# Three matmuls of 256 columns into one bank in place of 512 + 256 into two: the projections of a two-block transformer kernel

## The chip, the cores and the metric

One core of one Trainium2 chip runs the whole kernel. The metric is device time in microseconds. Before the change it is 3007.14 us, the median of three runs from 3000.47 to 3011.03. The engines are named as in the profile: PE is TensorE's matmul side, PEld its weight loads, DVE is VectorE, ACT is ScalarE, POOL is GpSimd, SP the engine that issues most DMAs.

## The reference, cut to what matters

The input is one sequence of 256 tokens with 2048 features, in fp32. The first block has a recurrent branch (width 2816), 16 heads of stick-breaking attention, a gated mixture, a feed-forward part of width 5632 and a gated extra input; then come two hybrid layers with differential attention, dilated attention and a convolution branch. Nearly all arithmetic is products of the 256 tokens with large weight matrices:

```
proj = h @ w_in[i]                                   # 2048 x 15872
y_r = ... @ w_rnn_out[i];  y_a = ... @ w_attn_out[i];  x = x + mix @ w_o[i]
gu = h @ w_ffn_gu[i];  x = x + (silu(g) * u) @ w_ffn_down[i]
ple_gate = sigmoid(rmsnorm(x, g_ple[i]) @ w_ple_gate[i])
proj = x @ w_in                                      # in each of the two hybrid layers
y = concatenate([ya, yb, yc], -1) @ w_out
```

All of them are to be right to more than one matmul in the fast fp32 format gives, so weights and activations are split.

## The kernel before

Activations lie with features on the 128 partitions and the 256 tokens (T) along the free side. The weight stream is cut in units: four k-tiles of 128 rows by 256 output columns (COLS), 512 KB, which SP loads into one of four slots of RAW. ACT makes the high part, WH, by a copy in the format fp32r (L594), DVE the low part, WL = RAW - WH (L1065), or POOL in a few units (L508). The activations in XH and YH are kept as two halves of 512 columns: columns 0 to 255 the high part, 256 to 511 the low part (L1090).

A group is 256 output columns over all k. For each k-tile and each half j of 128 output columns, PE does two matmuls with 128x128 stationary weights: WH against all 512 columns of x (L1755), and WL against the 256 high columns (L1757). The second adds into the upper half of the same bank, so a bank ends with WH*x_high in its lower 256 columns and WH*x_low + WL*x_high in its upper 256. The half j has a bank of its own; with two groups in turns (par) all four banks of the tile PG are used. When a group is complete, DVE evacuates it (L1078): a sum over the two halves of both banks, 1024 values per partition in, 512 out. PE waits, before it opens a group, for the evacuation of the group two before it (s_evac), and before each unit for WL (s_lo); where the activations of a phase are fresh, for them too (s_op).

The phases follow one another in the order of the program: attn (4 turns of 6 groups), gate_a, attn_out, x_r, gate_r, g_r, rnn_out, w_o, three pairs gu and down, ple, and for each of the two layers conf, dil, diffa, diffb, outa, outb and ln. Turn 0 of a phase is written out, the others run in a loop of the engine. Between groups a hook issues the small matmuls of attention, norms and the block-diagonal gates (L1851) into another tile, PX; transposes are L1779 and L1910. Nothing reorders instructions; each engine runs its own list, and semaphores tie them.

The stored program of PE has 10,459 matmuls before and 15,435 after; the hardware trace lists each with its weight load, and loops repeat them.

Of the kernel before, what the change touches and what calls it, by code (L numbers as in the profile page):

```python
# [23 lines left out]
T = 256  # L24
# [160 lines left out]
def program(nc, A, turns, real):  # L185
# [4 lines left out]
    AX = mybir.AxisListType.X  # L190
    ctx = ExitStack()
    with ctx:
        def sb(name, shape, dt=fp):
            return ctx.enter_context(nc.sbuf_tensor(name, shape, dt))
# [3 lines left out]
        WH = sb("WH", [P, SLOTS, UK, COLS], fr)  # L198
        WL = sb("WL", [P, SLOTS, UK, COLS], fr)
# [13 lines left out]
        PG = ctx.enter_context(nc.psum_tensor("PG", [P, 4, 512], fp))  # L213
# [120 lines left out]
        for l in range(2):  # L334
# [13 lines left out]
            out = [Group(wo, DC, 0, 0, YH, part=slice(1, U), closes=False),  # L348
                   Group(wo, DC, COLS, 0, YH, part=slice(1, U), closes=False, ahead=1),
                   Group(wo, DC, 0, 0, YH, part=slice(0, 1), opens=False, seen=2 * U - 1),  # L350
                   Group(wo, DC, COLS, 0, YH, part=slice(0, 1), opens=False)]
# [73 lines left out]
        s = Semaphores(*(ctx.enter_context(nc.semaphore("s_" + name)) for name in NAMES))  # L425
# [616 lines left out]
        def _(dve):  # L1042
            c = Counts(dve, "dve", turns, real)
            V_ = nc.vector
# [27 lines left out]
            def evacuate(grp, dst=None):  # L1072

                par = c.n.get("group", 0) % 2

                dve.wait_ge(s.unit, c.next("seen", grp.seen))
                out = G[:, par, :, :] if dst is None else dst
                V_.reduce_sum(out, PG[:, 2 * par:2 * par + 2, :].rearrange("p b (h t) -> p b t h", h=2), AX)\  # L1078
                    .then_inc(s.evac, 1)
                c.add("group")  # L1080
                dve.wait_ge(s.evac, c.value("group"))
                return Gf[:, par, :]
# [20 lines left out]
            def a_q(grp, i):  # L1103
                evacuate(grp, two(QR[:, 0, :]))

            def a_k(grp, i):
                evacuate(grp, two(QR[:, 1, :]))
                from_act()
                done(V_.scalar_tensor_tensor(QR[:, 0, :], QR[:, 0, :], der(D_QG), SQ2[:, 0, :], ALU.mult, ALU.mult))

            def a_v(grp, i):
                evacuate(grp)
                from_act()
                V_.scalar_tensor_tensor(QR[:, 1, :], QR[:, 1, :], vec("k_gain"), SQ2[:, 1, :], ALU.mult, ALU.mult)\
                    .then_inc(s.ready, 1)
                dve.wait_ge(s.ready, c.next("ready"))
# [614 lines left out]
        def _(pe):  # L1731
            c = Counts(pe, "pe", turns, real)
            mm = nc.tensor.matmul

            def group(grp, fresh=(), mid=None):


                par = (c.n.get("group", 0) + grp.ahead) % 2
                if grp.opens and c.n.get("group", 0) >= 2:

                    pe.wait_ge(s.evac, c.value("group", grp.ahead - 1))
                units = grp.units()
                for n, (k0, nk) in enumerate(units):
                    slot = c.n.get("unit", 0) % SLOTS

                    pe.wait_ge(s.lo, c.value("unit", 1))
                    if n < len(fresh) and fresh[n]:

                        pe.wait_ge(s.op, c.next("op", fresh[n]))
                    for kk in range(nk):  # L1750
                        x = grp.X[:, grp.base + k0 + kk, :]
                        for j in range(2):
                            b = 2 * par + j
                            cs = slice(P * j, P * j + P)
                            mm(PG[:, b, :], WH[:, slot, kk, cs], x, start=grp.opens and n == 0 and kk == 0,  # L1755
                               stop=False)
                            last = mm(PG[:, b, T:2 * T], WL[:, slot, kk, cs], x[:, 0:T], start=False,  # L1757
                                      stop=grp.closes and n == len(units) - 1 and kk == nk - 1)
                    last.then_inc(s.unit, 1)
                    c.add("unit")  # L1760
                    if mid and n in mid:
                        mid[n]()
                if grp.closes:
                    c.add("group")
# [230 lines left out]
            for q in range(DC // 2):  # L1995
# [7 lines left out]
                for e in range(2):  # L2003
                    for b in range(NB):
                        at = T * e + P * b
                        src = D * b + P * (2 * q + e)
                        last = nc.tensor.transpose(PG[:, q % 4, at:at + P], Fv[:, src:src + P], IDENT)
                last.then_inc(s.tp, 1)
                if q == 7:
                    ready()  # L2010
                    for b in range(NB):
                        last = mm(PX[:, 0, P * b:P * b + P], ONES, Gf[:, 1, P * b:P * b + P], start=True, stop=True)
                    last.then_inc(s.ss, 1)
            for ph in phases:
                if ph.name in between:
                    between[ph.name]()
                    continue
                hook = after.get(ph.name)

                def turn(i):  # L2020
                    for j, grp in enumerate(ph.body):
                        first = isinstance(i, int) and i == 0
                        group(grp, ph.fresh.get(j, ()) if first else (),
                              {0: diff_sum} if j == 1 and ph.name[:4] == "outa" else None)
                        if hook:
                            hook(i, j)
                turn(0)
                c.loop(1, ph.n, turn)

            for q in range(DC // 2):  # L2030
# [5 lines left out]
                for e in range(2):  # L2036
                    for b in range(NB):
                        at = T * b + P * e
                        last = nc.tensor.transpose(PG[:, q % 4, at:at + P], XRES[:, 2 * q + e, P * b:P * b + P],
                                                   IDENT)  # L2040
# [27 lines left out]
```

## Time and profile before

| | |
|---|---|
| median of the runs | 3007.14 us |
| span of the profiled execution | 3001.7 us |
| PE busy | 2922.9 us, 97% |
| PE's weight loads busy | 2534.9 us, 84% |
| DVE busy | 2130.3 us, 71% |
| ACT busy | 1411.3 us, 47% |
| POOL busy | 421.6 us, 14% |
| mean granted clock of PE | 0.989 of full speed |

The profiled execution's own time, what lies around its span included, is not listed apart; the three runs lie 1.2 us below to 9.3 us above its span. A busy PE is not a PE at its peak: durations of matmuls overlap, because the next starts while the pipeline of the last one drains. What a matmul costs is read from one start to the next.

### The profile page before, as it was taken

How to read it: one execution, taken by the hardware profiler on the slowest of the kernel's cores; microseconds unless marked ns; L12 is line 12 of the kernel's file. 1: busy time of each engine (PE TensorE's matmuls, PEld its weight loads, DVE VectorE, ACT ScalarE, POOL GpSimd, SP SyncE). 2: the span in 40 equal slices, each digit the busy share in tenths (PEclk: the TensorE clock that was granted, in tenths of full speed). 3: DMA queues.
4: the chain of work that ended last, by engine and by line, in shares of the span. 5: the costliest groups of instructions: out<-in, count | busy, mean ns of one | idle time of the engine just before them, and what ended most of it. 6: DMA issues, size and time to landing. Idle time of an engine off the chain costs nothing.

```text
span 3001.7 us, 45154 instructions
## 1 busy us (share of the span) xinstructions
PE 2922.9 (97%) x16516; PEld 2534.9 (84%) x16516; DVE 2130.3 (71%) x2372; ACT 1411.3 (47%) x1671; POOL 421.6 (14%) x382
## 2 busy tenths in 40 slices
PE   7999999999999999999999999999999997999997
PEld 6888888888888888888888888888888886888786
DVE  6666656776677677766666667776887786797777
ACT  5666643346654444443443344544444545434453
POOL 1000000203010000000000000116921100980110
PEclk9999999999999999999999999999999998999998
DMA  5545556653456556666565565565554554555453
GB/s 182 165 147 165 161 179 193 203 186 115 126 182 190 184 191 201 189 195 192 170 196 179 187 192 180 181 193 179 168 178 147 166 182 127 172 176 177 134 168 112
DMA packets 516869, 518.39 MB, mean 173 GB/s; under 512 B 17425, under 2 KB 514685, under 8 KB 516733
## 3 DMA queue, kind: packets, MB, share of 16 engines
q1 hardware_dynamic: 512357, 508.32, 54.1%
q0 software_dynamic: 3296, 5.56, 0.7%
q10 hardware_dynamic: 1080, 2.69, 0.3%
q8 instruction: 86, 1.41, 0.2%
q14 instruction: 50, 0.41, 0.0%
HBM read 514.39 MB, written 2.12 MB: 172 GB/s over the span
## 4 chain that ended last, share of the span: by engine, by line
PE 59%; DVE 9%; ACT 3%; issue 2%; DVEq 0%; POOL 0%; ACTq 0%; POOLq 0%
PE PG L1755 38%; PE PG L1757 19%; DVE WL L1065 3%; ACT WH L594 1%; DVE G L1078 1%; DVE MIX L1507 1%; DVE MIX L1394 0%; DVE F L1078 0%; DVE XRES L1606 0%; DVE TT L1618 0%; DVE TT L1235 0%; PE PX L1803 0%; ACT YH L685 0%; ACT L746 0%; DVE MIX L1725 0%
## 5 line engine op out<-in xcount | busy, mean ns | idle before, releaser
L1755 PE MATMUL PG<-XH,WH 128*128 128x512 f32 x4864 | 1733.8, 401 | 32.7 <-DVE XH L1090 23.2
L1065 DVE TENSOR_TENSOR WL<-RAW,WH 128x1024 fp32r<-128x1024 f32 (+1 forms) x944 | 1131.7, 1232 | 451.6 <-ACT WH L594 441.7
L1757 PE MATMUL PG<-XH,WL 128*128 128x256 f32 x4864 | 1364.6, 281 | 0.0
L594 ACT ACTIVATE WH<-RAW 128x1024 fp32r<-128x1024 f32 (+1 forms) x972 | 992.3, 1049 | 781.8 <-PE PG L1757 549.7
L1755 PEld LDWEIGHTS PG<-XH,WH 128*128 128x128 f32 x4864 | 917.5, 189 | 263.2 <-issue 35.0
L1755 PE MATMUL PG<-YH,WH 128*128 128x512 f32 x2848 | 1000.9, 396 | 7.2 <-DVE YH L1090 3.7
L1757 PEld LDWEIGHTS PG<-XH,WL 128*128 128x128 f32 x4864 | 922.1, 190 | 4.6 <-issue 4.1
L1757 PE MATMUL PG<-YH,WL 128*128 128x256 f32 x2848 | 796.4, 280 | 0.0
L1755 PEld LDWEIGHTS PG<-YH,WH 128*128 128x128 f32 x2848 | 534.1, 188 | 135.7 <-issue 9.5
L1757 PEld LDWEIGHTS PG<-YH,WL 128*128 128x128 f32 x2848 | 537.3, 189 | 1.3 <-issue 1.2
L1078 DVE TENSOR_REDUCE G<-PG 128x512 f32<-128x1024 f32 x198 | 241.2, 1218 | 36.7 <-PE PG L1757 36.6
L508 POOL TENSOR_TENSOR WL<-RAW,WH 128x1024 fp32r<-128x1024 f32 x28 | 67.4, 2407 | 1122.0 <-ACT WH L594 1063.6
L523 POOL MEMSET AL<- 128x1024 f32 x22 | 21.2, 965 | 674.3 <-DVE G L1078 507.9
L557 POOL TENSOR_SCALAR F<-MIX,VEC 128x256 f32<-128x256 f32 x56 | 78.8, 1407 | 0.0
L557 POOL TENSOR_SCALAR MIX<-MIX,VEC 128x256 f32<-128x256 f32 x56 | 73.5, 1312 | 5.5
L1394 DVE SCALAR_TENSOR_TENSOR MIX<-MIX,VEC 128x256 f32<-128x256 f32 x120 | 63.0, 584 | 6.4 <-DVE F L1420 1.9
L565 POOL TENSOR_TENSOR RT<-RT,F 128x256 f32<-128x256 f32 x56 | 62.8, 1122 | 0.0
L1851 PE MATMUL PX<-F,AL 128*128 128x256 f32 x280 | 61.7, 379 | 0.0
L1851 PEld LDWEIGHTS PX<-F,AL 128*128 128x128 f32 x280 | 52.6, 190 | 7.2
L821 ACT ACTIVATE F<-F,DER 128x128 f32<-128x128 f32 x64 | 29.2, 457 | 58.7 <-DVE DER L1409 57.6
L685 ACT ACTIVATE XH<-TT 128x512 f32 (+1 forms) x22 | 13.9, 632 | 89.4 <-DVE TT L1293 89.4
L565 POOL TENSOR_TENSOR RT<-RT,MIX 128x256 f32<-128x256 f32 x56 | 50.1, 895 | 4.7
(261 smaller groups left out, 1499.0 us busy)
## 6 DMA issues: line engine op xcount, KB each, us to landing
RAW<-in_w_in_dram SPq DMA_DIRECT2D x488, 512.0 KB, 4.7
RAW<-in_w_ffn_gu_dram SPq DMA_DIRECT2D x176, 512.0 KB, 4.6
RAW<-in_w_ffn_down_dram SPq DMA_DIRECT2D x88, 512.0 KB, 4.6
RAW<-in_w_out_dram SPq DMA_DIRECT2D x64, 512.0 KB, 4.6
RAW<-in_w_rnn_out_dram SPq DMA_DIRECT2D x40, 512.0 KB, 4.5
RAW<-in_w_attn_out_dram SPq DMA_DIRECT2D x32, 512.0 KB, 4.5
RAW<-in_w_o_dram SPq DMA_DIRECT2D x32, 512.0 KB, 4.7
RAW<-in_w_ple_gate_dram SPq DMA_DIRECT2D x32, 512.0 KB, 4.8
```

The costliest lines, as they stand in the source:

```text
L508: nc.gpsimd.tensor_tensor(WL[:, slot, :, :], RAW[:, slot, :, :], WH[:, slot, :, :].bitcast(fp), ALU.subtract).then_inc(s.lo, 1)
L557: ins = nc.gpsimd.tensor_scalar(to, HC[:, ch, tap + 2:tap + 2 + T], vec("conv_dw_2", (l * TAPS2 + tap) * CONVC + ch), None, ALU.mult)
L565: ins = nc.gpsimd.tensor_tensor(CB[:, ch, :], CB[:, ch, :], PT[ch % 2], ALU.add)
L594: nc.scalar.activation(WH[:, u % SLOTS, 0:nk, :], RAW[:, u % SLOTS, 0:nk, :], ACT.Copy)\
L821: last = nc.scalar.activation(S4[:, x, lo:up], S4[:, x, lo:up], ACT.Exp, bias=der(D_RED + 2 * x + b), accum_out=der(D_RED + 8 + 2 * x + b))
L1065: V_.tensor_tensor(WL[:, u % SLOTS, 0:nk, :], RAW[:, u % SLOTS, 0:nk, :], WH[:, u % SLOTS, 0:nk, :].bitcast(fp), ALU.subtract).then_inc(s. ...
L1078: V_.reduce_sum(out, PG[:, 2 * par:2 * par + 2, :].rearrange("p b (h t) -> p b t h", h=2), AX)\
L1394: ins = V_.scalar_tensor_tensor(CA[:, ch, :], src, vec("conv_dw_2", at), CA[:, ch, :], ALU.mult, ALU.add)
L1507: ins = V_.scalar_tensor_tensor(CA[:, ch, :], CA[:, ch, :], vec("conv_ln_g_2", CONVC * l + ch), PN[:, T:2 * T], ALU.mult, ALU.mult)
L1755: mm(PG[:, b, :], WH[:, slot, kk, cs], x, start=grp.opens and n == 0 and kk == 0, stop=False)
L1757: last = mm(PG[:, b, T:2 * T], WL[:, slot, kk, cs], x[:, 0:T], start=False, stop=grp.closes and n == len(units) - 1 and kk == nk - 1)
L1851: last = mm(PX[:, j % 4, T * m:T * m + T], BDS[:, i % 8, m, at:at + P], XC[:, i, :], start=i == users[j][0], stop=i == users[j][-1])
```

## The change

PG's one bank per group takes both halves: half j has columns 256 j to 256 j + 255. The matmul of WH against 512 columns is written as two of 256 columns, high part and low part of x, both into the same 256 columns of the bank, and WL against the high part adds there too. Only the very first matmul of a group opens the bank. The evacuation is a copy of 512 values instead of a sum over 1024. Banks 2 and 3 are no longer used by the groups.

```
-                V_.reduce_sum(out, PG[:, 2 * par:2 * par + 2, :].rearrange("p b (h t) -> p b t h", h=2), AX)\
-                    .then_inc(s.evac, 1)
+                V_.tensor_copy(out, two(PG[:, par, :])).then_inc(s.evac, 1)
...
+                        end = grp.closes and n == len(units) - 1 and kk == nk - 1
                         for j in range(2):
-                            b = 2 * par + j
+                            to = PG[:, par, T * j:T * j + T]
                             cs = slice(P * j, P * j + P)
-                            mm(PG[:, b, :], WH[:, slot, kk, cs], x, start=grp.opens and n == 0 and kk == 0,
-                               stop=False)
-                            last = mm(PG[:, b, T:2 * T], WL[:, slot, kk, cs], x[:, 0:T], start=False,
-                                      stop=grp.closes and n == len(units) - 1 and kk == nk - 1)
+                            mm(to, WH[:, slot, kk, cs], x[:, 0:T],
+                               start=grp.opens and n == 0 and kk == 0 and j == 0, stop=False)
+                            mm(to, WH[:, slot, kk, cs], x[:, T:2 * T], start=False, stop=False)
+                            last = mm(to, WL[:, slot, kk, cs], x[:, 0:T], start=False, stop=end and j == 1)
```

On PE, at the head of the loop of the attention phase (PG is the accumulator, XH the activations, WH and WL the high and low weights; the first row is the loop's wait for the evacuation), there stands before:

```order
L1746 ISA [waits s_evac]
L1755 MATMUL PG<-XH,WH 128x512 [waits s_lo]
L1757 MATMUL PG<-XH,WL 128x256
L1755 MATMUL PG<-XH,WH 128x512
L1757 MATMUL PG<-XH,WL 128x256
```

and now:

```order
L1745 ISA [waits s_evac]
L1755 MATMUL PG<-XH,WH 128x256 [waits s_lo]
L1757 MATMUL PG<-XH,WH 128x256
L1758 MATMUL PG<-XH,WL 128x256
L1755 MATMUL PG<-XH,WH 128x256
L1757 MATMUL PG<-XH,WH 128x256
L1758 MATMUL PG<-XH,WL 128x256
```

Three matmuls stand where two stood, each with a weight load of its own; the waits are the same. The body of this loop has 450 rows before and 643 after, and is the longest of all loops.

On DVE, in the same loop, around the evacuation of a group (F is its target), before:

```order
L1065 TENSOR_TENSOR WL<-RAW,WH 128x1024 [waits s_hi]
L1078 TENSOR_REDUCE F<-PG 128x512 [waits s_unit]
L1081 REGISTER_ALU
L1070 REGISTER_ALU [waits s_evac]
L1109 SCALAR_TENSOR_TENSOR F<-F,DER 128x512 [waits s_act]
```

and now:

```order
L1065 TENSOR_TENSOR WL<-RAW,WH 128x1024 [waits s_hi]
L1078 COPY F<-PG 128x512 [waits s_unit]
L1080 REGISTER_ALU
L1070 REGISTER_ALU [waits s_evac]
L1108 SCALAR_TENSOR_TENSOR F<-F,DER 128x512 [waits s_act]
```

Only the kind of the instruction changes there; nothing is moved on DVE, and ACT, POOL and SP have the same lists as before.

## Rows read from the trace of the kernel before

**Rows 1.** The page: span and busy time of each engine.
```profile
span 3001.7 us, 45154 instructions
PE 2922.9 (97%) x16516; PEld 2534.9 (84%) x16516; DVE 2130.3 (71%) x2372; ACT 1411.3 (47%) x1671; POOL 421.6 (14%) x382
```

**Rows 2.** Costliest groups: shapes, count | busy us, mean ns | idle before.
```profile
L1755 PE MATMUL PG<-XH,WH 128*128 128x512 f32 x4864 | 1733.8, 401 | 32.7 <-DVE XH L1090 23.2
...
L1757 PE MATMUL PG<-YH,WL 128*128 128x256 f32 x2848 | 796.4, 280 | 0.0
```

**Rows 3.** The chain that ended last, by engine and by line.
```profile
PE 59%; DVE 9%; ACT 3%; issue 2%; DVEq 0%; POOL 0%; ACTq 0%; POOLq 0%
PE PG L1755 38%; PE PG L1757 19%; DVE WL L1065 3%; ACT WH L594 1%; DVE G L1078 1%; DVE MIX L1507 1%; DVE MIX L1394 0%; DVE F L1078 0%; DVE XRES L1606 0%; DVE TT L1618 0%; DVE TT L1235 0%; PE PX L1803 0%; ACT YH L685 0%; ACT L746 0%; DVE MIX L1725 0%
```

**Rows 4.** PE's timeline near 1000 us: start us, duration us.
```profile
1000.04 0.40 PE L1755 MATMUL PG<-YH,WH 128*128 128x512 f32 x1
1000.29 0.28 PE L1757 MATMUL PG<-YH,WL 128*128 128x256 f32 x1
1000.41 0.40 PE L1755 MATMUL PG<-YH,WH 128*128 128x512 f32 x1
...
1005.71 0.40 PE L1755 MATMUL PG<-YH,WH 128*128 128x512 f32 x1
```

**Rows 5.** PE's timeline near 450 us.
```profile
450.07 0.28 PE L1757 MATMUL PG<-YH,WL 128*128 128x256 f32 x1
450.19 0.39 PE L1755 MATMUL PG<-YH,WH 128*128 128x512 f32 x1
450.42 0.27 PE L1757 MATMUL PG<-YH,WL 128*128 128x256 f32 x1
450.53 0.40 PE L1755 MATMUL PG<-YH,WH 128*128 128x512 f32 x1
...
455.74 0.39 PE L1755 MATMUL PG<-YH,WH 128*128 128x512 f32 x1
```

**Rows 6.** PE's waits: waited for: us in total, times, longest us.
```profile
PE PG L1755 <- DVE XH L1090: 23.2, 3, 11.2
PE PG L1755 <- DVE WL L1065: 12.1, 7, 5.0
PE PX L1910 <- DVE F L1459: 9.2, 2, 4.6
...
PE PG L1755 <- DVE YH L1090: 3.7, 2, 1.9
```

**Rows 7.** PE's timeline before a stall at 2314 us.
```profile
2314.56 0.28 PE L1757 MATMUL PG<-XH,WL 128*128 128x256 f32 x1
2319.46 0.90 PE L1910 MATMUL PX<-MATS,F 128*128 128x128 f32 x3 [4.62 <-DVE F L1459]
```

**Rows 8.** Durations of the two lines, ns: min/median/max, first and last start.
```profile
L1755 PE MATMUL PG<-YH,WH x2848: 391/395/799, 441.2 to 2971.1; 128*128 128x512 f32 x190
...
L1757 PE MATMUL PG<-YH,WL x2848: 274/280/284, 441.4 to 2971.3; 128*128 128x256 f32 x190
```

**Rows 9.** PE's timeline in the stretch at half clock, 28 us.
```profile
28.53 0.63 PE L1755 MATMUL PG<-XH,WH 128*128 128x512 f32 x1
28.96 0.41 PE L1757 MATMUL PG<-XH,WL 128*128 128x256 f32 x1
29.17 0.63 PE L1755 MATMUL PG<-XH,WH 128*128 128x512 f32 x1
```

**Rows 10.** A line of matmuls in true fp32.
```profile
L1851 PE MATMUL PX<-F,AL 128*128 128x256 f32 x280 | 61.7, 379 | 0.0
```

**Rows 11.** PE's weight loads near 2115 us: ten loads for ten transposes.
```profile
2115.43 0.69 PEld L1910 LDWEIGHTS PX<-MATS,F 128*128 128x128 f32 x6
2116.09 0.47 PEld L1779 LDWEIGHTS PX<-MATS,G 128*128 128x128 f32 x4
2116.53 0.19 PEld L1755 LDWEIGHTS PG<-XH,WH 128*128 128x128 f32 x1
```

**Rows 12.** DVE's evacuations and two kinds of copies from PSUM.
```profile
L1078 DVE TENSOR_REDUCE G<-PG 128x512 f32<-128x1024 f32 x198 | 241.2, 1218 | 36.7 <-PE PG L1757 36.6
...
L1078 DVE TENSOR_REDUCE F<-PG 128x512 f32<-128x1024 f32 x40 | 48.6, 1215 | 0.0
L1078 DVE TENSOR_REDUCE MIX<-PG 128x512 f32<-128x1024 f32 x12 | 14.6, 1219 | 0.1
...
L1637 DVE COPY XRES<-PG 128x512 f32<-128x512 f32 x8 | 5.5, 692 | 9.7 <-PE PG L2007 9.7
L1119 DVE COPY F<-PX 128x512 f32<-128x512 f32 x8 | 5.5, 692 | 0.3
```

**Rows 13.** PE in the phase g_r: stretch, busy (matmuls), clock, DMA, GB/s.
```profile
835.00:905.00 70.00, 69.59 (x388) 1.00 0.57 182
```

**Rows 14.** DMA queue of instruction fetches: packets, MB, share.
```profile
q8 instruction: 86, 1.41, 0.2%
```

**Rows 15.** DMA issues of the first weights: count, size, us to landing.
```profile
RAW<-in_w_in_dram SPq DMA_DIRECT2D x488, 512.0 KB, 4.7
```

## The prediction

> **What bounds the kernel now.** I read the page from the top. PE is busy 97% of a 3001.7 us span, DVE 71%, ACT 47% [rows 1]. The table of costly groups shows that nearly all of PE's time is two lines, L1755 (512 moving columns against WH) and L1757 (256 against WL), 4864 + 2848 = 7712 of each [rows 2]. The chain of waits gives PE 59%, those two lines 57%, with the split L1065 at 3% and the evacuation L1078 at 1% behind them [rows 3]. So I need what one pair of matmuls costs from start to start, not the printed durations, which overlap. The timeline gives it: 16 pairs from 1000.04 to 1005.71 us, 354 ns each [rows 4], and 16 pairs from 450.19 to 455.74, 347 ns each [rows 5]. The kernel alternates between these two rhythms, whatever DVE and ACT do; I take 350. 7712 x 0.350 = 2699 us, 90% of the span. Stalls are few: the list of who waited for whom has 23.2 us in 3 waits for XH, 12.1 in 7 for WL, 9.2 in 2 for F, 3.7 in 2 for YH [rows 6]; one row of the timeline is such a wait, 4.62 us [rows 7].
>
> **The change, PE's part.** Per k and half: before one WH load, 512 columns, one WL load, 256 columns. After: WH load, 256, the same WH load again, 256, WL load, 256. Moving columns stay 768; loads and matmuls go from two each to three each, so 7712 of both are added. The sum is therefore 7712 x (three 256-column steps - 350 ns).
>
> What is a 256-column step worth? Start to start it is 0.11 or 0.12 us, and a 512-column one 0.23 to 0.25 [rows 4, 5]. Finer: the durations have medians 395 and 280 ns [rows 8]; if both contain the same pipeline tail c, then 395 + 280 - 2c = 350, c = 162.5, and the steps are 232 and 117 ns. Minimum and maximum of L1757, 274 and 284, give 111 and 121. So three steps are 351 ns, bounds 333 and 364; against 350 that is +1 ns, +8 us, with ends -130 and +110 us. I take +8 since the median is where the rows lie, and the two ends are single steps of a rhythm that never stay (111 follows 118 or so).
>
> Is the step of 117 a real price of 256 columns when three come in a row? Three things in the rows speak for it. It already contains a load of WH behind it, and the load starts as the matmul starts. It does not shrink or grow when nothing follows: the last L1757 before a stall of almost 5 us lasts the same 0.28 [rows 7]. And it is in proportion: 256 columns more cost 232 - 117 = 115 ns, as much as the first 256, so next to nothing is left as a fixed price per matmul. At half clock (1.2 GHz, at 28 to 29 us) the steps are 0.43 and 0.21, which is one column per cycle with no extra [rows 9]; at 2.4 GHz 768 columns would be 320 ns, so the 30 ns above that are a limit that shows only at the full clock. If it is by column the change is free; if it is by matmul, it is a rival (below). True-fp32 matmuls of 256 columns, two passes each, last 379 ns, so 216 with the tail off, against 213 of pure columns [rows 10]: a matmul with its load need not cost more than 3 ns extra.
> The Trainium skill says, under TensorE: Matmul & The Clock Gate, Part 1, that a warm matmul carries about 2.5 ns on top of its columns. By that rule the added matmul alone costs 7712 x 2.5 ns, an estimate of +19 us, where the steps of the rows give +8; the true-fp32 rows agree with the size.
>
> Accumulation: WL's 256 columns already follow at once on WH's last 256 into the same place of the bank, so three in a row on one place add no nearer pair of writes. The banks: group and next group still use different ones, and what PE waits for before it opens a group (two groups back) is the same.
>
> Loads: three in 350 ns. Ten transposes in a row, each with its load of 128 columns, start 0.11 us apart [rows 11], so a load fits in 109 to 110 ns and hides in 117. If that cover were gone, each load would show whatever it exceeds 117 by; nothing here shows such an excess.
>
> **DVE's part.** The evacuation becomes a copy of 512 from one bank in place of a sum of 1024 over two. There are 250 (198 + 40 + 12) at 1.218 us; copies of 128x512 from PG and PX take 0.692 [rows 12]. That takes 0.526 us from each, 131 us of DVE work. Almost all of it lies beside PE's matmuls and is worth nothing. It is worth something in two places. First, in the stalls at phase ends, where the last evacuation stands ahead of what PE waits for: of the 14 waits just named, the two for F and the one of 11.2 us at the start have none in front [rows 6], which leaves 11, 11 x 0.5 = 5 us. Second, where the chain runs from evacuation to activation to the next split and PE is just short of work: from 835 to 905 us PE ran 388 matmuls in 70 us, 361 ns a pair [rows 13], so 11 ns above the rhythm; over the eleven groups of g_r, 352 pairs, that is 4 us, and 0.526 per group (5.8 us in all) covers it. Late next there is PE's own rhythm. Sum -9 us, bounds 0 (all hidden behind the next wait) and -20 (the stalls of 48 us in rows 6 lose one evacuation each, and some splits come earlier too).
>
> **Instruction fetch.** The program's matmuls go from 10,459 to 15,435. The fetch queue moved 86 blocks, 1.41 MB, in the whole run [rows 14]. That is 67 bytes for each of the stored 2 x 10,459 loads and matmuls but 43 for each of the 2 x 16,516 executed; I read it as the program fetched once, with loops running from what is held. All loops but one stay, after the change, below the 450-row body of the attention loop of before; that one grows to 643 rows. If it no longer fitted, its three turns would each fetch anew: at about 5 us from issue to landing, as the weights need [rows 15], no more than 15 us. The cost I take is 0.
> The Trainium skill (Runtime: NRT & Kernel Launch, Instruction fetch mechanics) gives PE room for 2048 instructions, in blocks of 256; 86 blocks hold 22,016, which agrees with the program once. By it 643 rows with their loads, near 1290, still fit. No run here shows the limit.
>
> **The sum.** +8 - 9 + 0 = -1 us against 3001.7 of span; the median of the runs is 3007.1, 5.4 above that span, and runs spread over 10 us, so I forecast 3005.
>
> **Rivals.**
> 1. A fixed price per matmul or weight swap. If the 30 ns above 320 are 15 per matmul, and the recorded starts hide it, a triple is 320 + 45 = 365: +15 x 7712 = +116 us, 3120. For it: the extra exists only at the full clock, where a load and the columns compete for less time. Against it: 232 against 117 is in proportion, and true-fp32 matmuls carry 3 ns. It ends slower; it decides from a fixed part of about 2 ns on (2 x 7712 = 15 us). Chance 0.17.
> 2. PE's sequencer. Six instructions per 350 ns are 58 each, before four, 88 each. Twenty (ten loads, ten transposes) took 1.10 us, 55 each [rows 11], limited perhaps by the array, so the sequencer can do 58 but the margin is unknown for longer runs. At 62 ns each the triple is 372, +22 x 7712 = +170 us, 3175. Chance 0.06. The Trainium skill (TensorE: Matmul & The Clock Gate, Part 1) has about 62 ns per MATMUL when the sequencer decodes in software; if this held for loads also, it is this case, and the 55 in the trace speaks against it.
> 3. The steps settle lower. There is a rhythm of 347 now in half the places; equal steps could lock there or at 3 x 115 = 345 throughout: -5 x 7712 = -39 us, and -9 of DVE, 2957. For it: the rhythm is regular to the nanosecond and depends on order. Against it: nothing says that the equal steps take the better one. Chance 0.15.
> 4. The relief of DVE is worth nothing, since each stall ends with ACT's or a weight's part; then +8 stands alone, 3013. This is within my own case.
>
> **Chances.** My case (steps of 115.5 to 118, so PE between -27 and +31 us, DVE -9) has 0.62; it is 2975 to 3035 by itself, likeliest 3005. A difference under 0.3% (9 us) cannot be told from none. Within my case faster, same and slower are 0.21, 0.25 and 0.16. With rival 3 faster is 0.36; with 1 and 2 slower is 0.39; same 0.25. The range holds my case, rival 3 and most of rival 1: 2955 to 3120.
>
> **What would show it.** Right: starts of L1755, L1757 and L1758 0.11 to 0.12 apart, three of them 0.345 to 0.355; durations near 280 on all three lines; L1078 at 0.69 us; DVE near 66% busy; the fetch queue near 126 blocks. In g_r the pair at 350. Rival 1 or 2: steps of 0.12 to 0.124, durations of 285 or more, and for rival 2 loads that start well after the matmul before them. Refetching: far more than 126 blocks. Wrong altogether: PE's clock leaving 2.4 GHz more often than the few short stretches of now, or new stalls for WL.

## The result and the profile after

The changed kernel takes 3059.53 us (median of four runs, 3057.14 to 3061.33) against 3006.83 us before (four runs of it by now): a ratio of 1.0184, 95% interval 1.0165 to 1.0204, so about 55 us slower. The forecast was 3005 us, which is no change, with a range of 2955 to 3120. The time lies in the range, and the slowdown was missed, though of the three chances the one for slower, 0.39, was the largest.

Three words recur below. A step is the time from one matmul's start to the next one's; a pair is the two matmuls of the kernel before, a triple the three of the changed one, each for one k-tile and one half of the output columns.

The page after: span and busy times (they answer to [rows 1]), the fetch queue ([rows 14]), the chain ([rows 3]), one of the groups of matmuls ([rows 2]) and DVE's evacuation ([rows 12]).

```profile
span 3059.5 us, 60578 instructions
...
PE 2993.1 (98%) x24228; PEld 2958.3 (97%) x24228; DVE 2006.9 (66%) x2372; ACT 1419.4 (46%) x1671; POOL 426.2 (14%) x382
...
q8 instruction: 125, 2.05, 0.3%
...
PE 68%; DVE 4%; ACT 1%; issue 1%; ACTq 0%; DVEq 0%
PE PG L1755 22%; PE PG L1758 22%; PE PG L1757 22%; DVE MIX L1506 1%; DVE XRES L1605 0%; DVE TT L1617 0%; PE PX L1803 0%; PE PX L1910 0%; PE PX L1901 0%; PE PX L1773 0%; DVE WL L1065 0%; PE PX L1779 0%; ACT WH L594 0%; PE PX L1804 0%; PE PX L1887 0%
...
L1757 PE MATMUL PG<-YH,WH 128*128 128x256 f32 x2848 | 805.9, 283 | 0.0
...
L1078 DVE COPY G<-PG 128x512 f32<-128x512 f32 x198 | 135.6, 685 | 45.8 <-PE PG L1758 45.8
```

DVE has lost 123 us of work, near the 131 expected, and the chain now runs through PE for 68% where it was 59%, and through DVE for 4% where it was 9%: the relief is there. A 256-column matmul lasts 283 ns in the mean, 3 ns more than the 280 of [rows 2]. The timeline of the changed kernel's PE (start us, duration us) gives the step from start to start:

```profile
471.04 0.28 PE L1755 MATMUL PG<-YH,WH 128*128 128x256 f32 x1
471.16 0.28 PE L1757 MATMUL PG<-YH,WH 128*128 128x256 f32 x1
471.28 0.28 PE L1758 MATMUL PG<-YH,WL 128*128 128x256 f32 x1
471.40 0.28 PE L1755 MATMUL PG<-YH,WH 128*128 128x256 f32 x1
...
472.84 0.28 PE L1755 MATMUL PG<-YH,WH 128*128 128x256 f32 x1
```

Fifteen steps in 1.80 us are 120.0 ns each, 360.0 a triple, and so it is in every undisturbed stretch of the program. The pair of before lasts 350.2 on average over the undisturbed stretches of its trace. So the 3 ns of each step over the 117 that I had read make the loss: 7712 x (360.0 - 350.2) = +76 us, less what the lighter evacuation gives back. The same stretch, 470 to 640 us, where both kernels run projections without a gap, shows it by counting; before, it is one of those with the faster rhythm, 347, so the difference is 13 ns there and not 10 (columns: stretch, busy us and number of matmuls, clock, DMA share, GB/s). Before:

```profile
470.00:640.00 170.00, 170.00 (x982) 1.00 0.63 194
```

and after:

```profile
470.00:640.00 170.00, 170.00 (x1420) 1.00 0.63 189
```

491 pairs before, 346 ns each, and 473 triples after, 359 (each count holds a few matmuls that hang over an edge). The clock is full in both; the loss is not a slower clock.

At half clock the changed kernel pays nothing extra, as before ([rows 9]): steps of 0.21 and 0.22 us, one column per cycle.

```profile
28.96 0.41 PE L1758 MATMUL PG<-XH,WL 128*128 128x256 f32 x1
29.17 0.41 PE L1755 MATMUL PG<-XH,WH 128*128 128x256 f32 x1
29.38 0.41 PE L1757 MATMUL PG<-XH,WH 128*128 128x256 f32 x1
29.60 0.41 PE L1758 MATMUL PG<-XH,WL 128*128 128x256 f32 x1
```

### The profile page after: what moved, and what is told of

It reads as the page before. It is cut to its first block, busy times and chain, and to the rows that moved or that the text cites. A ratio compares the mean times of both kernels' runs of the same rounds, so it can differ in the third digit from the quotient of the medians.

```text
span 3059.5 us, 60578 instructions
## 1 busy us (share of the span) xinstructions
PE 2993.1 (98%) x24228; PEld 2958.3 (97%) x24228; DVE 2006.9 (66%) x2372; ACT 1419.4 (46%) x1671; POOL 426.2 (14%) x382
## 4 chain that ended last, share of the span: by engine, by line
PE 68%; DVE 4%; ACT 1%; issue 1%; ACTq 0%; DVEq 0%
PE PG L1755 22%; PE PG L1758 22%; PE PG L1757 22%; DVE MIX L1506 1%; DVE XRES L1605 0%; DVE TT L1617 0%; PE PX L1803 0%; PE PX L1910 0%; PE PX L1901 0%; PE PX L1773 0%; DVE WL L1065 0%; PE PX L1779 0%; ACT WH L594 0%; PE PX L1804 0%; PE PX L1887 0%
## 5 line engine op out<-in xcount | busy, mean ns | idle before, releaser
L1755 PE MATMUL PG<-XH,WH 128*128 128x256 f32 x4864 | 1395.1, 287 | 27.8 <-DVE XH L1089 23.0
L1757 PE MATMUL PG<-XH,WH 128*128 128x256 f32 x4864 | 1380.8, 284 | 0.0
L1758 PE MATMUL PG<-XH,WL 128*128 128x256 f32 x4864 | 1380.7, 284 | 0.0
L1755 PEld LDWEIGHTS PG<-XH,WH 128*128 128x128 f32 x4864 | 938.5, 193 | 35.3 <-issue 32.0
L1757 PEld LDWEIGHTS PG<-XH,WH 128*128 128x128 f32 x4864 | 938.4, 193 | 4.8 <-issue 4.3
L1758 PEld LDWEIGHTS PG<-XH,WL 128*128 128x128 f32 x4864 | 938.0, 193 | 0.0
L1755 PE MATMUL PG<-YH,WH 128*128 128x256 f32 x2848 | 809.4, 284 | 3.8 <-DVE YH L1089 3.4
L1758 PE MATMUL PG<-YH,WL 128*128 128x256 f32 x2848 | 806.0, 283 | 0.0
L1757 PE MATMUL PG<-YH,WH 128*128 128x256 f32 x2848 | 805.9, 283 | 0.0
L1755 PEld LDWEIGHTS PG<-YH,WH 128*128 128x128 f32 x2848 | 546.7, 192 | 6.3 <-issue 5.5
L1757 PEld LDWEIGHTS PG<-YH,WH 128*128 128x128 f32 x2848 | 546.7, 192 | 1.3 <-issue 1.2
L1758 PEld LDWEIGHTS PG<-YH,WL 128*128 128x128 f32 x2848 | 546.7, 192 | 0.0
L1078 DVE COPY G<-PG 128x512 f32<-128x512 f32 x198 | 135.6, 685 | 45.8 <-PE PG L1758 45.8
```

The costliest lines, as they stand in the source:

```text
L1078: V_.tensor_copy(out, two(PG[:, par, :])).then_inc(s.evac, 1)
L1755: mm(to, WH[:, slot, kk, cs], x[:, 0:T], start=grp.opens and n == 0 and kk == 0 and j == 0, stop=False)
L1757: mm(to, WH[:, slot, kk, cs], x[:, T:2 * T], start=False, stop=False)
L1758: last = mm(to, WL[:, slot, kk, cs], x[:, 0:T], start=False, stop=end and j == 1)
```

## The experiments

**Which part of the change it is.** Two runs take the change apart. The first keeps the two banks and the sum, and only splits the matmul:

```
-mm(PG[:, b, :],        WH[..., cs], x,          start=..., stop=False)
+mm(PG[:, b, 0:T],      WH[..., cs], x[:, 0:T],  start=..., stop=False)
+mm(PG[:, b, T:2 * T],  WH[..., cs], x[:, T:2 * T], start=False, stop=False)
 last = mm(PG[:, b, T:2 * T], WL[..., cs], x[:, 0:T], ...)
```

> The matmul split alone: three matmuls of 256 columns, but into the two banks per group of the kernel before, and with its evacuation (a sum over 1024). In the changed kernel every step from one matmul's start to the next is 120 ns, 360 for a triple, where the pair took 350. If the price lies in the split (theories: a fixed part per matmul, a limit per weight load, a limit per instruction), the triple is 360 here too: 7625 to 7712 times 10 ns is +76 us, and since nothing is relieved on DVE the time is 3070 to 3085, slower than the changed kernel by what the lighter evacuation is worth (5 to 20 us). If the price lies in the accumulator (three matmuls in a row onto the same 256 columns of one bank), the triple falls back to 350 here and the time to 3000 to 3012.

Measured: 3069.47 us against 3003.51 before, ratio 1.0224 (1.0206 to 1.0242), and the steps are 120 ns here too, 1419 matmuls where the changed kernel has 1420:

```profile
470.00:640.00 170.00, 170.00 (x1419) 1.00 0.62 188
```

So the accumulator has no part in it; the split does it. The second run keeps the pair and only makes the evacuation light:

```
-V_.reduce_sum(out, PG[:, 2 * par:2 * par + 2, :].rearrange("p b (h t) -> p b t h", h=2), AX)
+V_.tensor_copy(out, two(PG[:, 2 * par, :]))
```

> The evacuation alone: the pair of matmuls of the kernel before, with a copy of 512 values from one bank in place of the sum over two (what the second half holds is left out). It shows what the relief of DVE is worth where PE has its old rhythm. By the prediction -9 us, so 2998; if all of it hides behind other waits 0; the rhythm of PE stays 347 or 353 ns a pair. If it moves more than 20 us, the relief also changes PE's rhythm.

Measured: 2989.87 us against 3003.51, ratio 0.9955 (0.9937 to 0.9974), 13.5 us faster (8 to 19). PE's waits in it, which answer to [rows 6]:

```profile
PE PG L1754 <- DVE XH L1089: 22.6, 3, 11.2
...
PE PG L1754 <- DVE WL L1065: 7.7, 4, 4.0
...
PE PX L1909 <- DVE F L1458: 7.3, 2, 3.6
...
PE PG L1754 <- DVE YH L1089: 3.7, 2, 1.9
```

48.2 us of such waits have become 41.3. And in g_r, where [rows 13] has 388 matmuls in 70 us, there are now 396, 354 ns a pair and not 361, which over 352 pairs is 2.6 us:

```profile
835.00:905.00 70.00, 69.94 (x396) 1.00 0.57 182
```

This run also shows that the rhythm of the pair is not a property of the place. From 470 to 640 us it has 965 matmuls, 352 ns a pair, where the run of before has 982, and from 1720 to 1800 it has 463 where the run of before has 455:

```profile
470.00:640.00 170.00, 170.00 (x965) 1.00 0.64 194
...
1720.00:1800.00 80.00, 80.00 (x463) 1.00 0.62 189
```

**What a step is made of.** A fixed price per matmul, a floor per weight load (a step can't be shorter than its load), or a floor per instruction: all three give 120. The next runs change one size at a time. First, the second matmul of each triple with half the moving columns:

```
-mm(to, WH[..., cs], x[:, T:2 * T], start=False, stop=False)
+mm(PG[:, par, T * j:T * j + 128], WH[..., cs], x[:, T:T + 128], start=False, stop=False)
```

> The changed kernel, with the second matmul of each triple (WH against the low part of x) cut to 128 moving columns; the other half of the tokens misses that product. Fixed part per matmul (columns at 2.4 GHz plus 13.3 ns, which gives 120 for 256 and 226.7 for 512): its step falls to 53.3 + 13.3 = 67 ns, the triple to 307, the time by 411 us to about 2650, as far as other engines let it. Limit per weight load (a step with a load of 128 columns can't be under 120) or per instruction (60 ns each): steps stay at 120, triple 360, time 3059.

Measured: 2994.29 us, a triple of 349 to 353 ns, by the stretch:

```profile
470.00:640.00 170.00, 170.00 (x1464) 1.00 0.63 194
...
900.00:1100.00 200.00, 200.00 (x1700) 1.00 0.61 191
```

Neither theory's number: 128 columns less save 7 to 11 ns, not 53 and not 0. The timeline shows why the three steps must be taken together:

```profile
449.90 0.28 PE L1755 MATMUL PG<-YH,WH 128*128 128x256 f32 x1
450.02 0.22 PE L1757 MATMUL PG<-YH,WH 128*128 128x128 f32 x1
450.08 0.34 PE L1758 MATMUL PG<-YH,WL 128*128 128x256 f32 x1
450.26 0.28 PE L1755 MATMUL PG<-YH,WH 128*128 128x256 f32 x1
```

L1758 is printed as starting 0.06 us after L1757, and then "lasts" 0.34 where it lasts 0.28 elsewhere. So its start was recorded early. That it then stood waiting for its load is likely, since e5 below has 112 ns from load to load, but it is not shown. In a stream of unequal matmuls the printed starts and durations move time from one to the other; only the sum is right.

Next, the same second matmul with 64 columns of weights in place of 128:

```
+mm(PG[0:64, par, T * j:T * j + T], WH[:, slot, kk, P * j:P * j + 64], x[:, T:2 * T], start=False, stop=False)
```

> The changed kernel, with the second matmul of each triple loading only 64 columns of WH as weights (64 of 128 output features get the product with the low part of x), still 256 moving columns. Fixed part per matmul: all steps stay 120. Limit per instruction: all stay 120. Limit per weight load: the step that hides this half load is no longer held by it and falls towards the 107 to 109 ns that 256 columns take, so the triple to about 347 and the time by 95 us to about 2965.

Measured: 2993.41 us, triple 350.0.

```profile
470.00:640.00 170.00, 170.00 (x1459) 1.00 0.63 195
```

The width of the load matters with moving columns and instructions unchanged, but this is a mixed stream again. So the following runs make all three matmuls alike (the first and last k-tile of a group keep their shapes):

```
+w_, m_ = (P, T) if first or last k-tile else (128, 128)     # then (64, 256), (64, 128), (32, 256)
+to = PG[0:w_, par, T * j:T * j + m_];  cs = slice(P * j, P * j + w_)
 mm(to, WH[..., cs], x[:, 0:m_]);  mm(to, WH[..., cs], x[:, T:T + m_]);  mm(to, WL[..., cs], x[:, 0:m_])
```

> The changed kernel with all three matmuls of a triple cut to 128 moving columns (the first and last k-tile of a group keep their shapes; the other half of the tokens misses the products), weights still 128 columns. The two runs before it left two theories: a floor per weight load, about 116 ns for 128 columns (W), and a floor per instruction, about 58 ns, two per step (I). Both expect steps of about 116, a triple near 349, though the columns alone would take 53 ns. If instead the steps fall to 70 or less, the price goes with the moving columns.

Measured: 3017.3 us; steps 111.7 ns (335.0 a triple), not the 116 of either theory.

```profile
449.94 0.27 PE L1761 MATMUL PG<-YH,WL 128*128 128x128 f32 x1
450.05 0.27 PE L1758 MATMUL PG<-YH,WH 128*128 128x128 f32 x1
450.16 0.27 PE L1760 MATMUL PG<-YH,WH 128*128 128x128 f32 x1
450.27 0.28 PE L1761 MATMUL PG<-YH,WL 128*128 128x128 f32 x1
```

With 128 weight columns a step doesn't fall below 112 ns, though its moving columns would take 53. That lies under 120: loads could keep up with the changed kernel. It also accounts for e3, whose triple would be 120.0 + 111.7 + 120.0 = 351.7, between the 349 and 353 measured. The mean clock of this run was 0.948 and not 0.989, which costs it time outside these steps, so its total says nothing on them.

> The changed kernel with all three matmuls loading 64 columns of weights, 256 moving columns each (half of the output features are not computed). W: loads take 60 ns or so and the moving columns decide: 107 to 109 ns a step, a triple of 320 to 327. I: still 116 a step, 349. If both the load and the columns get in each other's way, something between.

Measured: 2940.77 us; the durations of one line (ns, min/median/max):

```profile
L1760 PE MATMUL PG<-YH,WH x2848: 276/276/283, 434.1 to 2909.0; 128*64 128x256 f32 x163, 128*128 128x256 f32 x27
```

Uniform streams settle the tail of a duration too: 283 for a step of 120.0, so 163, and this median is a step of 113.3, 340.0 a triple. It is not 107 to 109, as theory W (a floor per load) had it, and not 116, as theory I (a floor per instruction) had it. 6.7 ns over the columns are left of 13.3. In e4 one such step beside two full ones should give 353.3; it had 350.0, and why is open. Half the weight columns also means results for half the partitions; no run separates the two.

> The changed kernel with 64 columns of weights and 128 moving columns in all three matmuls (three quarters of the products are left out). W: steps of 58 to 65 ns, since a half load takes about half. I: still 116, since there are two instructions in each step whatever their size. The time of the kernel will be set by DVE and ACT then, so the steps within a unit are what is read.

Measured: 2569.59 us; steps of 60 ns where PE doesn't wait. The total can't be compared, since PE now often waits for other engines and its mean clock is 0.903.

```profile
1251.73 0.22 PE L1760 MATMUL PG<-YH,WH 128*64 128x128 f32 x1
1251.79 0.22 PE L1761 MATMUL PG<-YH,WL 128*64 128x128 f32 x1
1251.85 0.22 PE L1758 MATMUL PG<-YH,WH 128*64 128x128 f32 x1
1251.91 0.22 PE L1760 MATMUL PG<-YH,WH 128*64 128x128 f32 x1
```

Two instructions, a load and a matmul, in 60 ns: a floor of 58 ns per instruction is out. And 60 is again the columns at 2.4 GHz, 53.3, and 6.7.

The next run goes the other way, from the kernel before: WL's matmul gets all 512 columns of x, so that every step moves 512.

```
-last = mm(PG[:, b, T:2 * T], WL[..., cs], x[:, 0:T], ...)
+last = mm(PG[:, b, :],       WL[..., cs], x,         ...)
```

> The kernel before with the WL matmul over all 512 columns of x (one product more than the result needs), so that PE runs 512 and 512, with a load of 128 columns under each. No load can be late there. If a 512-column step is its columns and a small fixed part, it is 213 + 3 = 216, the pair 432; if the step of 230 to 235 seen in the kernel before is the column rate of this format, the pair is 460 to 470; if what is added to the columns is paid per load (13 to 17 ns each), 453 to 460. Against 350 the first adds 630 us to the time, the second 850 to 925.

Measured: 3763.01 us; pairs of 453.3 in every undisturbed stretch, 226.7 a step. The durations and the count:

```profile
L1757 PE MATMUL PG<-YH,WL x2848: 387/389/402, 548.5 to 3730.7; 128*128 128x512 f32 x190
...
470.00:640.00 170.00, 170.00 (x753) 1.00 0.46 144
```

This is the run that decides. 512 columns are 213.3 ns at 2.4 GHz and cost 226.7; 256 are 106.7 and cost 120.0. The extra is 13.3 ns in both. It is paid per matmul with its load of 128 weight columns, whether 256 or 512 columns move. Every matmul here has a load of its own, so what a matmul without one would pay isn't shown. The pair of before should then cost 226.7 + 120.0 = 346.7, which is the faster of its two rhythms (347 in [rows 5]).

The last of the uniform streams loads 32 weight columns per matmul.

> The changed kernel with all three matmuls of a triple loading 32 columns of weights, 256 moving columns each (three quarters of the output features are not computed, but for the first and last k-tile of a group). Steps so far at 256 moving columns: 120.0 ns with 128 weight columns, 113.3 with 64; the columns alone are 106.7. If the extra goes with the width of the load, a quarter load adds 3.3 ns, a step of 110.0, a triple of 330. If it is a fixed part of 6.7 per matmul plus something that only a full load adds, the step stays 113.3, a triple of 340.

Measured: 2979.66 us. In some stretches steps of 113.3, as with 64 columns, in others up to about 117.8, never 110:

```profile
L1760 PE MATMUL PG<-YH,WH x2848: 276/280/415, 436.3 to 2947.9; 128*32 128x256 f32 x163, 128*128 128x256 f32 x27
```

Both branches of the expectation miss; the extra is not in proportion to the width of the load. 128 weight columns cost 13.3, 64 cost 6.7, and 32 cost 6.7 to 11, no less than 64. Why is open.

**The slower rhythm of before, 353.3.** The uniform streams with 128 weight columns have one rhythm each, 335.0, 360.0 and 453.3; the pair of 512 and 256 has two. If that comes from alternating, another order of the same matmuls should help.

```
 for kk in range(nk):
-    for j in range(2):  WH matmul of j, WL matmul of j
+    for j in range(2):  WH matmul of j
+    for j in range(2):  WL matmul of j
```

> The kernel before, same matmuls and banks, in another order: per k-tile the two WH matmuls of 512 columns, then the two WL matmuls of 256, so sizes change half as often. The runs so far: a matmul costs its columns at 2.4 GHz plus 13.3 ns for a load of 128 weight columns (256: 120.0; 512: 226.7), which makes a pair 346.7; the kernel before runs part of its time at 353.3, which no uniform stream shows. If the extra 6.7 comes from alternating a long and a short matmul at each step, it is gone or halved: mean per pair 346.7 to 348.5, time 12 to 26 us below before. If it comes from something else (phase of the engine after a stall), the mean stays 350 and the time is that of before within 0.3%.

Measured: 2994.67 us against 3003.87, ratio 0.9972 (0.9962 to 0.9983). The pair is at 348.4 ns in every undisturbed stretch (350.2 on average in the run of before), inside the 346.7 to 348.5 foreseen; the gain of 8 us is below the 12 that it gave.

```profile
470.00:640.00 170.00, 170.00 (x978) 1.00 0.63 194
...
1720.00:1800.00 80.00, 80.00 (x461) 1.00 0.60 186
```

The next run sorts the whole unit (both loops over k inside the unit, first all WH, then all WL).

> The same with the whole unit sorted: eight WH matmuls of 512 columns, then eight WL matmuls of 256. Sizes change twice per unit of sixteen matmuls. Alternation theory: all pairs at 346.7 but for a few ns per unit, 24 to 26 us below before, 2977 to 2983, lower than the run sorted by twos if that one is only halved. Other theory: no change. WL is needed later in the unit, but the unit's one wait is for WL, so nothing is gained there.

Measured: 3001.3 us against 3003.87, ratio 0.9996 (0.9987 to 1.0005). The expectation of 2977 to 2983 fell. One unit of sixteen matmuls takes 2.79 us, 349 a pair, where 8 x 346.7 is 2.77:

```profile
1272.32 2.00 PE L1753 MATMUL PG<-YH,WH 128*128 128x512 f32 x8
1274.16 1.12 PE L1758 MATMUL PG<-YH,WL 128*128 128x256 f32 x8
1275.11 2.00 PE L1753 MATMUL PG<-YH,WH 128*128 128x512 f32 x8
```

With a quarter of the size changes of the order by twos it is slower than that one. So the extra beyond 13.3 per matmul doesn't go with the number of changes. With full loads it comes with unequal sizes alone, but e11, whose moving columns are all alike, has a slower rhythm as well, so unequal sizes are not its only source. One thing can be seen in the starts of e10's unit: the eight steps of 512 columns are 233, 236, 228, 233, 231, 226, 227 and 227 ns, the eight of 256 are 113, 119 and six of 120. A change of size is felt over several steps behind it. What sets it stays open. The order by twos is the only version that computes all the products and is faster than both kernels.

## Why the prediction was wrong

**The step worth of 256 columns** is the term that failed: "three steps are 351 ns ... +1 ns, +8 us". They are 360.0, +10 ns, and +76 us against the true mean of 350.2. I split the measured pair of 350 into 232 and 117 by its printed durations. e3 shows that in a mixed stream these shift between neighbours, and e8 with the changed kernel gives the true parts, 226.7 and 120.0 (and up to 6.7 for the mixture). A shift of 3 ns, multiplied by three matmuls and 7712, is 69 us, more than the 55 by which the time lies above the forecast; DVE's relief and shorter waits, below, took the rest back. The bounds of 333 and 364 held it; the median was the wrong value to take. The range held the time because it was drawn to hold most of rival 1: my own case ended at 3035.

**"It is in proportion"** was the argument that turned me from rival 1, and it was made of the same 3 ns. 232 to 117 looks like a price by column, 226.7 to 120.0 is a fixed 13.3. Rival 1, a fixed price per matmul or swap hidden by the recorded starts, is what happened, and I gave it 0.17. It was priced at 15, from 30 ns over 320 shared by two, and so at +116 us; but the fixed part is 13.3, and 3.5 of the 30 are the mean cost of mixing sizes, which the uniform triple doesn't pay. So it is +10 a triple and not +15. (The 3120 of rival 1 and the 3175 of rival 2 also leave out DVE's -9, which lies in no other term.) The true-fp32 row ([rows 10]), with 3 ns extra, was no witness for this format. Nor was the last L1757 before a stall ([rows 7]), which kept its 0.28: in the changed kernel the last one before each of its five longest stalls lasts 279 ns, where those in the stream last 283 at a step of 120.0. The duration in front of a stall doesn't tell the step. And that the 117 "already contains a load" was no reason to hold it for the columns' own, since half the load takes 6.7 ns off the step (e6).

The Trainium skill's rule that a warm matmul carries about 2.5 ns over its columns (TensorE: Matmul & The Clock Gate, Part 1) points the right way, with an estimate of +19 us. The trace disagrees with its size for this format: 13.3 ns per matmul with its full load (e8, and the changed kernel).

**At half clock nothing is paid.** That the 30 ns are a limit of the full clock was right; it told nothing between column and matmul, since both vanish there.

**Accumulation and banks:** right. e1, with the old banks, has the same 120 ns.

**Loads:** right that they fit, 112 ns a load (e5) against 120; the ten transposes ([rows 11]) had 110. But fitting is not free: with half the load the step is 113.3 (e6).

**DVE's part:** -9 us, bounds 0 and -20; e2 measured -13.5. The evacuation takes 0.685 against my 0.692. The changed kernel against e1, which differ by the two banks and the evacuation, says the same: 1.0184 against 1.0224. With it fell rival 4, by which the relief is worth nothing.

**Instruction fetch:** right. 125 blocks, 126 foreseen, so the loop of 643 rows is not fetched anew on its turns.

**The sum:** +76 - 13.5 = +62 us against 55 measured (50 to 61), and e1 has 67 of 76. About 8 us of the rhythm's price don't show in either. The spans of the profiled executions say where they are. What lies outside the 7712 pairs or triples at their rhythm is 3001.7 - 7712 x 0.3502 = 301 us before; by the same sum it is 294 in e1 (span 3069.9, triple 360.0), 289 in e2 (2990.9, pair 350.3) and 283 in the changed kernel. So the lighter evacuation takes 12 us out of it, the slower stream by itself 7, and the changed kernel, which has both, 18: where PE waits for others, slower steps give them time. One such place is g_r: in e1, where it comes later by the slower stretches before it, 576 matmuls in 70 us are 365 a triple where [rows 13] had 361 a pair, so 4 and not 10 ns are paid over 352 of them, 2 us.

```profile
845.00:915.00 70.00, 69.36 (x576) 1.00 0.56 179
```

The other places were not traced one by one.

**Rival 2**, a floor per instruction, fell with e7 (30 ns each); **rival 3**, a lower rhythm, with the changed kernel itself. Of the signs named ahead, the steps of 0.12 were those of rival 1; the durations, 283, lie between the 280 of my case and its 285.

## What to carry to other kernels

Before splitting a matmul that reuses its weights, price what each matmul with its load costs beside its columns, and take that from a uniform stream: in this format 13.3 ns, 11% of the step with 256 columns and 6% with 512. In a stream of unequal matmuls trust the sum of a period, never the printed share of each. When the likeliest value and a rival differ by a few ns times thousands, the forecast hangs on the rival's chance and not on the middle of the range.

## What the hardware showed beyond that

- Uniform streams in this format, full clock: 226.7 ns (512 moving, 128 weight columns), 120.0 (256, 128), 113.3 (256, 64), 60 (128, 64), 111.7 (128, 128), 113.3 to 117.8 (256, 32). At half clock 0.21 us for 256 (128), nothing extra.
- Alternating 512 and 256 columns gives 346.7 or 353.3 ns a pair, and which one holds in a phase is not fixed by the place: two runs with the same matmuls on PE, before and e2, have 982 and 965 of them in the same 170 us. The four runs of before beside the changed kernel spread over 11 us, the four of the changed kernel over 4.
- Printed starts of matmuls can be early by some 50 ns when a short one with a full load stands between long ones: e3 prints a step of 60, where e5, with the same load and columns throughout, has 112.
